# Expert matrices of a mixture layer: middle index numbered 11p + b, the last matrix read in rows of 12 KB

## The chip, the cores and the metric

The kernel runs on one core of a Trainium2 chip. The metric is the device time of one execution in microseconds. TensorE (PE in the profile) multiplies; its weight loads have a row of their own there (PEld). VectorE is DVE, ScalarE is ACT, GpSimd is POOL. SyncE (SP) issues all the weight loads of the part that is changed.

## The reference, cut to what matters

The program computes two layers of a hybrid trunk. The part that is changed is the feed-forward block of the second layer: a router picks two of eight experts for each of 256 tokens, and each expert is a SwiGLU with a middle width of 2816.

```python
def swiglu(h, w1, w3, w2):
    return jnp.matmul(jax.nn.silu(jnp.matmul(h, w1)) * jnp.matmul(h, w3), w2)

def moe_swiglu(h, router, w1, w3, w2):
    ...
    y = jnp.zeros_like(h)
    for e in range(N_EXPERTS):
        y = y + gates[..., e:e + 1].astype(h.dtype) * swiglu(h, w1[e], w3[e], w2[e])
    return y
```

`w1[e]` and `w3[e]` are 1024 x 2816 in float32, `w2[e]` is 2816 x 1024. The middle index (the 2816 columns of the first two, which are the 2816 rows of the last) is only summed over, so it may be taken in any order, as long as all three matrices use the same one.

## The kernel before

Everything up to the experts (two layers of mixing, the dense block of layer 0, the router) is left as it is. The experts run in a loop over rounds and, inside it, over the 8 experts; with these inputs there is one round. One expert is 24 pieces of weights, q = 0 to 23, that go through 8 slots `RAW` of 12 KB per partition, each with a slot `WLO` beside it:

- q 0 to 3 and 4 to 7: `w1` and `w3`, the first half of the middle index (1408 = 11 blocks of 128), two blocks of 128 rows of the matrix each, 128 x 2816 elements a piece; q 8 to 15: the same for the second half.
- q 16 to 23: `w2`, by `YBLOCKS`: six pieces of three blocks of 128 rows, then two of two blocks. A block has one row of 1024 floats (4 KB) in each partition.

For each piece, SP waits until the slot is free and issues the load (L1377 to L1393). DVE waits for the load and subtracts the upper half of each float, read as bfloat16 in place (`WHI`, every second 2-byte word), from the float; the rest goes to `WLO` as bfloat16 (L1547). PE then multiplies with both parts. DVE counts `m_lo` up for each piece and PE waits for it.

In `uv_piece` the weights of PE are 128 columns of the piece, one column of the middle index for each output row: `hi` columns lie 4 bytes apart, `lo` columns 2 bytes. There are 11 blocks x 2 rows x 3 products = 66 matmuls of 96 moving columns in a piece (L1429 and L1431 with `hi`, L1432 with `lo`), and 16 such pieces in an expert. In `y_piece` the hidden values are the weights (96 columns) and the piece is the moving operand, 512 columns at a time (L1451), 132 matmuls in an expert.

What else stands in the order: PE scatters the previous expert's output into token order after q 1 and q 3 (`pe_scatter`, L1409); DVE adds it to `Y` after its own q 3 and q 6 (`dve_add`, L1518). DVE forms the hidden values after q 9 and q 17 (`dve_hidden`, L1525 and L1527). PE gathers the next expert's tokens after q 17 (`pe_gather`, L1401). ACT copies the output (L1506) and takes silu (L1511). DVE copies a transposed gate and the next tokens after q 20 (L1565, L1496).

Of the kernel before, what the change touches and what calls it, by code (L numbers as in the profile page):

```python
# [35 lines left out]
P = 128  # L36
D = 1024
KC = D // P
# [84 lines left out]
def trunk(nc, t):  # L123
    ctx = ExitStack()
    with ctx:
# [35 lines left out]
        def B(i):  # L161
            return PS[:, i, :]
# [155 lines left out]
        for L in range(DEPTH):  # L318
# [4 lines left out]
            for g, key in enumerate(dict.fromkeys(u[0] for u in units)):  # L323
                c0, w = next((u[3], u[4]) for u in units if u[0] == key)
# [19 lines left out]
            if L == 0:  # L344
                for key in FFN_LOADS:
                    n = key[-1]
# [3 lines left out]
                    elif key[0] == "w2":  # L350
                        rows = min(4 * P, D_FF - 4 * P * n)
                        src = t["ffn_w2"][0][4 * P * n:4 * P * n + rows, :].rearrange("(c p) n -> p c n", p=P)
                        item(key, place, [(None, src)], ("ffn_y_mm", n + 1), split=True,
                             part=lambda v, r=rows // P: v[:, 0:2 * r, :])
                    else:
                        f0, w = FT[n]
# [883 lines left out]
        HALF, HB = D_FF // 2, FC // 2  # L1240
# [7 lines left out]
        HEH, HEL = HE[:, :, 0, :], HE[:, :, 1, :]  # L1248
# [96 lines left out]

        UBANK, VBANK, YBANK, GBANK, TBANK = 0, 3, 6, 0, 2
        GROUPS = [(0, 4), (4, 8), (8, HB)]
        YBLOCKS = [(3 * j, 3 * j + 3) for j in range(6)] + [(18, 20), (20, 22)]
        USED, FULL = 20, 12

        def uv_bank(bank0, b):

            return B(bank0 + b // 4)[:, SLOTS * (b % 4):SLOTS * (b % 4) + SLOTS]
# [21 lines left out]
        def sp_moe(sp):  # L1375
            for other in ENG:
                sp.wait_ge(S(f"{other}_stage_done"), MOE_STAGE)  # L1377

            def body(i, e):
                for q in range(NPIECE):  # L1380
                    sp_slot_free(sp, i, q)
                    if q < 16:
                        half, k = q // 8, 2 * (q % 4)
                        w = t["moe_w3" if q % 8 >= 4 else "moe_w1"][0, bass.ds(e, 1), P * k:P * k + 2 * P,
                                                                   HALF * half:HALF * half + HALF]
                        src = w.rearrange("a (k p) n -> p (a k) n", p=P)
                        dst = RAW[q % NSLOT][:, 0:2 * HALF].rearrange("p (k n) -> p k n", k=2)
                    else:
                        c0, c1 = YBLOCKS[q - 16]
                        w = t["moe_w2"][0, bass.ds(e, 1), P * c0:P * c1, :]  # L1390
                        src = w.rearrange("a (c p) n -> p (a c) n", p=P)
                        dst = RAW[q % NSLOT][:, 0:D * (c1 - c0)].rearrange("p (c n) -> p c n", n=D)
                    sp.dma_start(dst, src).then_inc(S(f"m_raw{q % NSLOT}"), 16)  # L1393
            rounds(sp, body)
# [25 lines left out]
        def pe_moe(pe):  # L1420
            def uv_piece(i, q, bank0):

                pe.wait_ge(S("m_lo"), NPIECE * i + q + 1)
                hi, lo = WHI[q % NSLOT], WLO[q % NSLOT]
                for n in range(2):
                    k = 2 * (q % 4) + n
                    for b in range(HB):
                        out, f = uv_bank(bank0, b), HALF * n + P * b
                        pe.matmul(out, hi[:, f:f + P], HEH[:, k, :], start=k == 0 and b % 4 == 0, stop=False,  # L1429
                                  skip_group_check=True)  # L1430
                        pe.matmul(out, hi[:, f:f + P], HEL[:, k, :], start=False, stop=False, skip_group_check=True)  # L1431
                        mm = pe.matmul(out, lo[:, f:f + P], HEH[:, k, :], start=False, stop=k == KC - 1,  # L1432
                                       skip_group_check=True)
                        if k == KC - 1 and b in (3, 7, HB - 1):
                            mm.then_inc(S("m_full"), 1)
                if q % 4 < 3:
                    mm.then_inc(S("m_used"), 1)
# [369 lines left out]
```

## Time and profile before

| | us |
|---|---|
| median of 3 runs | 2250.21 |
| lowest, highest | 2249.07, 2251.18 |
| profiled execution | 2252.25 |
| its span in the profile | 2250.5 |
| PE, DVE busy in the span | 1959.2, 1219.3 |
| the experts' part, first DVE piece to last PE piece | about 1532 to 2234 |
| one expert, from the third on | about 87.5 |

The times in the rows are microseconds from the start of the span, unless marked ns. A matmul's row lasts longer than its turn: the next one starts before it ends, so the turn is read from start to start. "Idle before" and the waits name what the engine waited for. The granted clock of PE is given as a share of 2.4 GHz. The chain at the page's end and the waits of one stretch serve to tell which engine holds the others up there.

### The profile page before, as it was taken

Reading aid. Unit: us, or ns where it says so; the run is one execution under the profiler, and the core shown is the slowest. Engines: PE = TensorE matmul, PEld = TensorE weight load, DVE = VectorE, ACT = ScalarE, POOL = GpSimd, SP = SyncE. Lnnn points to the kernel's source line nnn. Section 1 sums busy time; section 2 is a strip of 40 time slices with the busy share of each in tenths; the row PEclk is TensorE's granted clock in tenths of the full one; section 3 lists DMA queues with packets and bytes.
Section 4 is the critical chain, followed back from the end, with each engine's and each line's share of the span. In section 5 each row is a group of like instructions: output and inputs, shape, how many; then the busy total and the mean of one; then the engine's idle time right before and its main releaser. Section 6 shows DMA issues by size and latency. Waiting matters only on the chain.

```text
span 2250.5 us, 34491 instructions
## 1 busy us (share of the span) xinstructions
PE 1959.2 (87%) x15242; PEld 1248.2 (55%) x15242; DVE 1219.3 (54%) x1272; ACT 330.1 (15%) x555; POOL 177.0 (8%) x112
## 2 busy tenths in 40 slices
PE   2899997799779999797899858877999999999997
PEld 0333466756434444243444556646687687786774
DVE  1100327575352332222103475548999998989987
ACT  1200000043242222110100003321101101001000
POOL 0000505100000000000004450000000000000000
PEclk9899997855689999799999977578999999999999
DMA  8442210000144544412122100018999999999994
GB/s 275 174 169 103 74 49 1 1 1 1 38 150 169 202 153 161 175 57 75 38 75 75 56 0 1 1 38 360 411 411 413 410 399 396 410 397 401 404 390 162
DMA packets 121027, 409.34 MB, mean 182 GB/s; under 512 B 22168, under 2 KB 28952, under 8 KB 114736
## 3 DMA queue, kind: packets, MB, share of 16 engines
q1 hardware_dynamic: 112560, 405.57, 46.6%
q10 hardware_dynamic: 8320, 1.50, 0.6%
q8 instruction: 130, 2.13, 0.4%
q14 instruction: 17, 0.14, 0.0%
HBM read 406.01 MB, written 1.05 MB: 181 GB/s over the span
## 4 chain that ended last, share of the span: by engine, by line
PE 69%; DVE 18%; issue 5%; DMA 3%; ACTq 2%; ACT 2%; DVEq 1%; POOLq 1%; POOL 0%; PEldq 0%; SPq 0%; PEld 0%
PE PS L598 10%; PE PS L1165 10%; DVE ARENA L1547 10%; PE PS L596 8%; PE PS L1147 5%; PE PS L738 5%; PE PS L1429 4%; PE PS L1431 3%; PE PS L1432 3%; PE PS L1451 3%; PE PS L1084 3%; PE PS L969 2%; DMA ARENA<-in_moe_w 2%; ACTq L1645 2%; PE PS L445 2%
## 5 line engine op out<-in xcount | busy, mean ns | idle before, releaser
L1547 DVE TENSOR_TENSOR ARENA<-ARENA 128x2816 bf16<-128x2816 f32 (+1 forms) x192 | 581.5, 3084 | 5.8 <-DMA ARENA<-in_moe_w 3.8
L1429 PE MATMUL PS<-ARENA 128*128 128x96 bf16 x2816 | 376.1, 209 | 39.1 <-DVE ARENA L1547 33.4
L1431 PE MATMUL PS<-ARENA 128*128 128x96 bf16 x2816 | 375.4, 208 | 2.9 <-issue 2.9
L1432 PE MATMUL PS<-ARENA 128*128 128x96 bf16 x2816 | 375.4, 208 | 1.8 <-issue 1.7
L1429 PEld LDWEIGHTS PS<-ARENA 128*128 128x128 bf16 x2816 | 279.5, 99 | 53.3 <-DVE ARENA L1547 44.6
L1431 PEld LDWEIGHTS PS<-ARENA 128*128 128x128 bf16 x2816 | 279.7, 99 | 8.3 <-issue 8.3
L1432 PEld LDWEIGHTS PS<-ARENA 128*128 128x128 bf16 x2816 | 279.6, 99 | 3.1 <-issue 2.9
L1451 PE MATMUL PS<-ARENA 128*96 128x512 bf16 x1056 | 237.6, 384 | 2.9 <-DVE ARENA L1547 2.9
L598 PE MATMUL PS<-ARENA 128*128 128x512 f32 (+1 forms) x608 | 239.7, 554 | 0.0
L1165 PE MATMUL PS<-ARENA 128*128 128x512 bf16 x1056 | 232.6, 381 | 2.5 <-DVE ARENA L1197 2.5
L378 DVE TENSOR_TENSOR ARENA<-ARENA 128x4096 bf16<-128x4096 f32 (+1 forms) x26 | 91.4, 3522 | 227.5 <-ACT ARENA L372 227.4
L1451 PEld LDWEIGHTS PS<-ARENA 128*96 128x96 bf16 x1056 | 127.9, 122 | 106.4 <-issue 4.0
L629 DVE COPY ARENA<-PS 128x512 f32<-128x512 f32 (+1 forms) x32 | 19.9, 624 | 308.1 <-PE PS L598 308.1
L598 PEld LDWEIGHTS PS<-ARENA 128*128 128x128 f32 x608 | 116.2, 192 | 124.7 <-issue 121.4
L1165 PEld LDWEIGHTS PS<-ARENA 128*128 128x128 bf16 x1056 | 102.4, 98 | 136.0 <-issue 13.2
L596 PE MATMUL PS<-ARENA 128*128 128x512 f32 x384 | 169.7, 601 | 2.3 <-ACTq L395 2.3
L738 PE MATMUL PS<-ARENA 128*128 128x128 f32 x768 | 116.3, 326 | 53.6 <-issue 33.8
L738 PEld LDWEIGHTS PS<-ARENA 128*128 128x128 f32 x768 | 114.0, 241 | 56.3 <-issue 56.2
L596 PEld LDWEIGHTS PS<-ARENA 128*128 128x128 f32 x384 | 73.0, 192 | 97.5 <-issue 92.9
L1147 PE MATMUL PS<-ARENA 128*128 128x512 bf16 x528 | 117.0, 386 | 0.8 <-DVE GATE L483 0.8
L372 ACT ACTIVATE ARENA<-ARENA 128x4096 bf16<-128x4096 f32 (+1 forms) x26 | 74.9, 2890 | 149.1 <-PE PS L1147 85.5
L445 PE MATMUL PS<-ARENA,SC 128*32 128x512 f32 x384 | 48.9, 635 | 50.8 <-ACT SC L1650 44.0
(224 smaller groups left out, 1801.8 us busy)
## 6 DMA issues: line engine op xcount, KB each, us to landing
ARENA<-in_moe_w SPq DMA_DIRECT2D x128, 1408.0 KB, 12.9
ARENA<-in_moe_w SPq DMA_DIRECT2D x48, 1536.0 KB, 15.3
ARENA<-in_ada_w SPq DMA_DIRECT2D x24, 2048.0 KB, 7.7
ARENA<-in_ffn_w SPq DMA_DIRECT2D x15, 2048.0 KB, 7.9
ARENA<-in_w_in SPq DMA_DIRECT2D x12, 2048.0 KB, 8.0
ARENA<-in_moe_w SPq DMA_DIRECT2D x16, 1024.0 KB, 16.4
ARENA<-in_w_out SPq DMA_DIRECT2D x8, 1024.0 KB, 5.4
ARENA<-in_w_in SPq DMA_DIRECT2D x4, 1024.0 KB, 6.3
```

The lines of the kernel that those rows point to most:

```text
L378: dve.tensor_tensor(it["lo"], it["raw"], it["hi"], ALU.subtract).then_inc(S("split_lo"), 1)
L445: mm = pe.matmul(ps[32 * g:32 * g + 32, :], SC[:, 2 * kk + n, :], w[:, n, 512 * g:512 * g + 512], start=kk == 0 and n == 0, stop=False)
L596: mm = pe.matmul(B(bank), slot[:, k, P * u:P * u + P], HT[:, k, :], start=k == 0, stop=k == KC - 1)
L598: mm = pe.matmul(B(bank)[:, 0:w], HT[:, k, P * u:P * u + P], slot[:, k, 0:w], start=k == 0, stop=k == KC - 1)
L738: mm = pe.matmul(B(4 * d + h)[:, c], KE[d][:, h, c], q[:, h, c], start=True, stop=True)
L1147: mm = pe.matmul(B(2 * x + h), a[:, c, P * x:P * x + P], w[:, at:at + 512], start=c == 0 and n == 0, stop=c == FC - 1 and n == 2)
L1165: mm = pe.matmul(B(b0 + i % 3), w[:, k, P * c:P * c + P], x[:, k, :], start=k == 0 and w is hi and x is HTH, stop=k == KC - 1 and w is lo)
L1429: pe.matmul(out, hi[:, f:f + P], HEH[:, k, :], start=k == 0 and b % 4 == 0, stop=False, skip_group_check=True)
L1431: pe.matmul(out, hi[:, f:f + P], HEL[:, k, :], start=False, stop=False, skip_group_check=True)
L1432: mm = pe.matmul(out, lo[:, f:f + P], HEH[:, k, :], start=False, stop=k == KC - 1, skip_group_check=True)
L1451: mm = pe.matmul(B(YBANK + h)[0:SLOTS, :], x, y[:, at:at + 512], start=c == 0 and n == 0, stop=c == FC - 1 and n == 2)
L1547: dve.tensor_tensor(WLO[q % NSLOT][:, 0:n], RAW[q % NSLOT][:, 0:n], WHI[q % NSLOT][:, 0:n], ALU.subtract).then_inc(S("m_lo"), 1)
```

## The change

The 1408 middle indices of each half get another order. Before, block b held the 128 consecutive indices 128b to 128b + 127, index 128b + p in partition p. Now block b holds the indices 11p + b.

- For `w2`, partition p then needs rows 11p to 11p + 10 of the half, which lie one behind another in memory: 44 KB. A piece of three blocks is one run of 12 KB per partition, one of two blocks 8 KB, where before it was three or two runs of 4 KB. A piece may no longer reach over the border of the halves, so `YBLOCKS` becomes 3, 3, 3, 2 blocks in each half, in place of 3, 3, 3, 3, 3, 3, 2, 2.
- For `w1` and `w3` the loads stay. The weights of a matmul are now every 11th column of the piece: `hi` 44 bytes apart, `lo` 22 bytes.

The numbers of matmuls, DVE operations, loads and bytes are the same.

```diff
-        YBLOCKS = [(3 * j, 3 * j + 3) for j in range(6)] + [(18, 20), (20, 22)]
+        YBLOCKS = [(HB * half + a, HB * half + min(a + 3, HB)) for half in range(2) for a in range(0, HB, 3)]
...
                         c0, c1 = YBLOCKS[q - 16]
-                        w = t["moe_w2"][0, bass.ds(e, 1), P * c0:P * c1, :]
-                        src = w.rearrange("a (c p) n -> p (a c) n", p=P)
+                        half = c0 // HB
+                        w = t["moe_w2"][0, bass.ds(e, 1), HALF * half:HALF * half + HALF, :]
+                        src = w.rearrange("a (p c) n -> p (a c) n", p=P)[:, c0 - HB * half:c1 - HB * half, :]
...
-                        out, f = uv_bank(bank0, b), HALF * n + P * b
-                        pe.matmul(out, hi[:, f:f + P], HEH[:, k, :], start=k == 0 and b % 4 == 0, stop=False,
+                        out, f = uv_bank(bank0, b), slice(HALF * n + b, HALF * n + HALF, HB)
+                        pe.matmul(out, hi[:, f], HEH[:, k, :], start=k == 0 and b % 4 == 0, stop=False,
                                   skip_group_check=True)
-                        pe.matmul(out, hi[:, f:f + P], HEL[:, k, :], start=False, stop=False, skip_group_check=True)
-                        mm = pe.matmul(out, lo[:, f:f + P], HEH[:, k, :], start=False, stop=k == KC - 1,
+                        pe.matmul(out, hi[:, f], HEL[:, k, :], start=False, stop=False, skip_group_check=True)
+                        mm = pe.matmul(out, lo[:, f], HEH[:, k, :], start=False, stop=k == KC - 1,
                                        skip_group_check=True)
```

The order changes only at the pieces of `w2`. On PE, at the end of an expert's body (L1451 before and L1452 after are `y_piece`, L1401 and L1402 the gather; every number of a line below the diff's is one higher after). Before:

```order
L1451 MATMUL PS<-ARENA 96x512 x18
L1440 REGISTER_ALU
L1451 MATMUL PS<-ARENA 96x512 x18
L1440 REGISTER_ALU
L1451 MATMUL PS<-ARENA 96x512 x18
L1440 REGISTER_ALU
L1451 MATMUL PS<-ARENA 96x512 x18
L1440 REGISTER_ALU
L1451 MATMUL PS<-ARENA 96x512 x12
L1440 REGISTER_ALU
L1451 MATMUL PS<-ARENA 96x512 x12
```

After, the same six pieces behind the gather:

```order
L1452 MATMUL PS<-ARENA 96x512 x18
L1441 REGISTER_ALU
L1452 MATMUL PS<-ARENA 96x512 x12
L1441 REGISTER_ALU
L1452 MATMUL PS<-ARENA 96x512 x18
L1441 REGISTER_ALU
L1452 MATMUL PS<-ARENA 96x512 x18
L1441 REGISTER_ALU
L1452 MATMUL PS<-ARENA 96x512 x18
L1441 REGISTER_ALU
L1452 MATMUL PS<-ARENA 96x512 x12
```

One of the two short pieces has moved from fifth place (q 22) to second (q 19) of these six. On DVE, from the hidden values of the second half to the loop's end (L1547 and L1548 are the subtraction, L1565 and L1566 the gate's copy, L1496 and L1497 the tokens). Before:

```order
L1527 TENSOR_TENSOR ARENA<-ARENA 128x1056
L1547 TENSOR_TENSOR ARENA<-ARENA 128x3072 x3
L1565 COPY M<-PS 96x256
L1495 ISA
L1496 TENSOR_TENSOR ARENA<-PS,ARENA 128x4x96
L1495 REGISTER_ALU
L1496 TENSOR_TENSOR ARENA<-PS,ARENA 128x4x96
L1547 TENSOR_TENSOR ARENA<-ARENA 128x3072
L1547 TENSOR_TENSOR ARENA<-ARENA 128x2048 x2
```

After:

```order
L1528 TENSOR_TENSOR ARENA<-ARENA 128x1056
L1548 TENSOR_TENSOR ARENA<-ARENA 128x3072
L1548 TENSOR_TENSOR ARENA<-ARENA 128x2048
L1548 TENSOR_TENSOR ARENA<-ARENA 128x3072
L1566 COPY M<-PS 96x256
L1496 ISA
L1497 TENSOR_TENSOR ARENA<-PS,ARENA 128x4x96
L1496 REGISTER_ALU
L1497 TENSOR_TENSOR ARENA<-PS,ARENA 128x4x96
L1548 TENSOR_TENSOR ARENA<-ARENA 128x3072 x2
L1548 TENSOR_TENSOR ARENA<-ARENA 128x2048
```

The copy and the tokens stand one block (1024 elements) earlier than before.

## Rows read from the trace of the kernel before

**Rows 1.** The page, part 1: busy time, share of the span, instructions.

```profile
PE 1959.2 (87%) x15242; PEld 1248.2 (55%) x15242; DVE 1219.3 (54%) x1272; ACT 330.1 (15%) x555; POOL 177.0 (8%) x112
```

**Rows 2.** Busy time by stretch: one expert (the fifth), columns in the first line.

```profile
core 0: us, PE busy (x) PEld busy (x) DVE busy (x) ACT busy (x) POOL busy (x), PEclk, DMA share, GB/s
...
1877.80:1965.30 87.50, 82.48 (x1232) 65.77 (x1230) 81.75 (x44) 7.20 (x12) 0.00 (x0) 0.98 1.01 401
```

**Rows 3.** Waits, 1500 to 2250: engine, line, for what; us, times, longest.

```profile
DVE X L1518 <- PE PS L1409: 34.8, 14, 5.5
PE PS L1429 <- DVE ARENA L1547: 33.4, 22, 5.9
...
DVE ARENA L1547 <- DMA ARENA<-in_moe_w: 3.8, 10, 0.5
...
SPq L1393 <- PE PS L1432: 352.1, 124, 6.6
```

**Rows 4.** The same waits, only those for a DMA, 1530 to 1700.

```profile
DVE ARENA L1547 <- DMA ARENA<-in_moe_w: 3.4, 9, 0.5
```

**Rows 5.** DVE in order of time: start, length, operation, idle before.

```profile
1870.10 19.76 DVE L1547 TENSOR_TENSOR ARENA<-ARENA 128x3072 bf16<-128x3072 f32 x7
1895.37 0.69 DVE L1518 TENSOR_TENSOR X<-PS,X 128x512 f32<-128x512 f32 x1 [5.51 <-PE PS L1409]
...
1896.84 9.09 DVE L1547 TENSOR_TENSOR ARENA<-ARENA 128x2816 bf16<-128x2816 f32 x3
```

**Rows 6.** The same, one expert later.

```profile
1982.90 0.69 DVE L1518 TENSOR_TENSOR X<-PS,X 128x512 f32<-128x512 f32 x1 [5.47 <-PE PS L1409]
1983.76 0.69 DVE L1518 TENSOR_TENSOR X<-PS,X 128x512 f32<-128x512 f32 x1 [0.17 <-PE PS L1409]
1984.37 3.08 DVE L1547 TENSOR_TENSOR ARENA<-ARENA 128x2816 bf16<-128x2816 f32 x1
```

**Rows 7.** Busy time by stretch (columns as in rows 2) over that expert's chain.

```profile
1896.00:1941.00 45.00, 42.51 (x930) 40.27 (x928) 44.80 (x26) 2.57 (x6) 0.00 (x0) 1.00 1.01 401
1941.00:1972.00 31.00, 31.00 (x166) 17.60 (x166) 30.97 (x17) 2.27 (x3) 0.00 (x0) 1.00 1.02 409
1972.00:1974.50 2.50, 0.07 (x1) 0.00 (x0) 2.50 (x2) 2.36 (x3) 0.00 (x0) 1.00 1.00 394
```

**Rows 8.** PE in order of time, around the start of the next expert.

```profile
1974.56 0.21 PE L1429 MATMUL PS<-ARENA 128*128 128x96 bf16 x1 [2.48 <-DVE ARENA L1547]
...
1981.78 1.95 PE L1409 MATMUL PS<-GATE,M 96*128 96x512 f32 x4
1983.56 0.21 PE L1429 MATMUL PS<-ARENA 128*128 128x96 bf16 x1
```

**Rows 9.** PE, first and last of 69 matmuls in a row at the full clock.

```profile
1800.07 0.21 PE L1429 MATMUL PS<-ARENA 128*128 128x96 bf16 x1 [2.60 <-DVE ARENA L1547]
...
1802.96 0.21 PE L1432 MATMUL PS<-ARENA 128*128 128x96 bf16 x1
```

**Rows 10.** Durations by line, ns: min/median/max, first and last start, form.

```profile
L1429 PEld LDWEIGHTS PS<-ARENA x2816: 96/98/145, 1535.2 to 2202.2; 128*128 128x128 bf16 x188
...
L1432 PEld LDWEIGHTS PS<-ARENA x2816: 95/98/145, 1535.2 to 2202.2; 128*128 128x128 bf16 x188
...
L1451 PEld LDWEIGHTS PS<-ARENA x1056: 121/122/126, 1591.6 to 2233.4; 128*96 128x96 bf16 x176
L1451 PE MATMUL PS<-ARENA x1056: 377/387/429, 1591.6 to 2233.6; 128*96 128x512 bf16 x176
```

**Rows 11.** PE in order of time: 13 float32 matmuls of 128 columns, merged.

```profile
329.76 1.61 PE L738 MATMUL PS<-ARENA 128*128 128x128 f32 x13
```

**Rows 12.** Durations of line 738 on PE, ns: min/median/max.

```profile
L738 PE MATMUL PS<-ARENA x768: 274/275/553, 320.2 to 1348.4; 128*128 128x128 f32 x192
```

**Rows 13.** Busy time by stretch (columns as in rows 2): loads of w1, w3, then w2.

```profile
1530.00:1532.00 2.00, 0.00 (x0) 0.00 (x0) 0.39 (x1) 0.36 (x1) 0.00 (x0) 1.00 1.02 428
...
1888.00:1905.00 17.00, 17.00 (x299) 14.90 (x297) 11.32 (x6) 1.28 (x3) 0.00 (x0) 0.92 0.96 365
1905.00:1927.30 22.30, 21.10 (x489) 20.66 (x487) 22.27 (x13) 0.40 (x1) 0.00 (x0) 1.00 1.02 415
1927.30:1955.80 28.50, 27.21 (x369) 20.59 (x367) 28.47 (x17) 3.15 (x6) 0.00 (x0) 1.00 1.02 408
```

## The prediction

> **What bounds the kernel now.** The page's first part gives PE 87% of the span and DVE 54% [rows 1], an average over stages; only the experts are changed, so the first view to open is the busy time of one expert. In 87.5 us PE is busy 82.48, DVE 81.75, and the DMA share is 1.01 [rows 2]. Three resources look full, and the change touches two of them: it could give the DMA something and take something from PE. Which one sets the time is told by the waits. DVE waits for a load only 3.8 us in the whole stage [rows 3], 3.4 of it before 1700, that is in the first two experts [rows 4]; it waits 34.8 us for PE's scatter (L1409), and PE waits 33.4 us for DVE's subtraction. SP waits 352.1 us for slots that PE has not freed. So the loads are ahead: the DMA is busy because it runs nearly at the pace of the loop, but it doesn't set that pace.
>
> The order of time shows the loop. DVE idles 5.51 us before its add at 1895.37, then starts q 4 at 1896.84 [rows 5]; one expert later it idles 5.47 us before the add and starts q 4 at 1984.37 [rows 6]. That is 87.53 us from q 4 to q 4, in two parts. (a) 1896.8 to 1941: DVE works without a gap (44.80 of 45.00 us) and PE follows it [rows 7]. (b) 1941 to 1984: PE's w2 pieces, back to back for 31.0 us; 2.5 us in which PE goes round the loop [rows 7]; q 0 and q 1, 1974.56 to 1981.78; the scatter of 1.8 us; then DVE's two adds [rows 6, 8]. DVE has done its pieces 0 to 3 long before and waits. The chain is DVE for one half and PE for the other; no load is in it.
>
> **The turn of one matmul.** 69 matmuls of `uv_piece` start between 1800.07 and 1802.96 [rows 9]: 2.89 / 68 = 42.5 ns each, at the 2.4 GHz level. 96 moving columns at one per cycle are 40 ns. So the moving operand sets the turn and the weight load lies under it. A piece of 66 takes 2.8 us, against 3.0 for DVE's subtraction (9.09 us for three [rows 5]). This closeness is what the change puts at risk.
>
> **Part 1: w2 in runs of 12 KB.** The w2 loads of this expert took about 28.5 us at 408 GB/s; the stretch with w1 and w3, whose runs are 5.6 KB, shows 415 [rows 13]. The nearest row for a gain by longer runs is the step from 4 to 5.6 KB, 408 to 415: 0.5 us of an expert. The upper end is the best rate in any row, 428 in a short stretch: 28.5 x (1 - 408/428) = 1.3 us. The lower end is a loss, if 128 streams 44 KB apart read memory less well; the worst row of this stretch, 365 GB/s, would make 28.5 into 31.9, a loss of 3.4. I take a gain of 0.5 to 1 us of DMA time. On the path it is worth nothing, since no load is on it: even in the first two experts all of DVE's waits for a DMA are 3.4 us [rows 4], for the loads of all three matrices, and whatever DVE gains there ends before the wait for the scatter. Cover: the wait for PE's scatter, 5.5 us in each expert. **Value taken: 0.**
>
> **Part 2: pieces of w2 in another order.** A short piece moves from q 22 to q 19. The sum on PE and DVE is the same, and PE runs through (b) without a wait after the first 0.4 us. DVE's copy and tokens come one block, some 1.1 us, earlier; PE needs them 15 us later. SP's waits are by piece number and a slot is freed at most 1.4 us earlier or later. **0.**
>
> **Part 3: weights 44 and 22 bytes apart.** 1056 weight loads per expert, 8448 in all. No row of before has weights more than 4 bytes apart, so the price is bounded.
> - The rows within reach: `hi` (4 bytes) and `lo` (2 bytes) both take 98 ns [rows 10], so doubling the step cost nothing there. The w2 matmuls read the piece as moving operand: 387 ns, with a minimum of 377 [rows 10]. One product in three reads `lo` and two read `hi`, so I read the 10 ns as what the 4-byte step costs over 512 columns, an estimate: a step isn't always free.
> - How much room a load has: the load of 96 columns takes 122 ns, of 128 columns 98 [rows 10]. The 128-column form is thus a faster one. If 96 columns go one per cycle (40 ns), the fixed part is 82, and the fast load itself lasts about 16 ns (estimate). It may become 2.6 times as long before it reaches the turn of 42.5.
> - Lower end: nothing. Upper end: the float32 matmuls of L738, whose weights have no fast form. 13 of them take 1.61 us, the last one 0.275 [rows 11, 12]: (1.61 - 0.275) / 12 = 111 ns a turn. Half of it, 55.5 ns, is a plain load of 128 columns at one per cycle (53 ns) with the 2.5 ns that the turn of 42.5 has over its 40.
>
> From turn to time: let d be what the turn grows by. q 0 and q 1 (132 matmuls) lie in (b) and cost 132 d. The 14 pieces in (a) (924 matmuls) take 14 x 2.81 + 1.8 for a scatter = 41.1 of the 45.0 us, so 3.9 us are free; they cost 924 d - 3.9 us, if that is above nothing, that is from d = 4.2 ns on.
>
> Here the Trainium skill speaks on both sides. The SBUF page (SBUF — State Buffer, on SBUF "cachelines" in Door 1) says that the memory is read in lines of 16 bytes, that two hits on a line are needed to hide its latency, and that each access to a new line costs; both new steps put every weight on a line of its own. That rule speaks against the change; no run here shows its size. TensorE: Matmul & The Clock Gate (Weight-path perf modes) lets the fast load be used with columns up to 1,024 elements apart, and 22 is well inside; by that the fast form stays.
>
> I take the fast form as kept and its 16 ns as at most doubled, to 32: still under 42.5, so d = 0. The row it is nearest to is `hi` against `lo`, 98 and 98. **Value taken: 0.**
>
> **Sum.** 2252.25 us for the profiled execution, less 0, plus 0. The median of the runs is 2250.21, 2.0 lower than the profiled one, so I predict 2250.
>
> **The rivals.**
> - R1, slower: the load loses the fast form or runs at a quarter of it, and the turn becomes 55.5 ns. d = 13.0: 132 d = 1.7, 924 d - 3.9 = 8.1; 9.8 us per expert, 79 us: 2329. For it: a new line for each weight, and 10 ns seen in the moving operand at only 4 bytes. Against: the ratio of 2.6 that the load has to spare. It decides from d = 4.2 ns, a turn of 46.7.
> - R2, much slower: the slower memory adds to a plain load, or the four parts of a fast load get in each other's way, and the turn is the 111 ns of L738. d = 68.5: 9.0 + 59.4 = 68.4 us per expert, 547 us: 2797. PE would never wait and DVE would wait for it at every piece.
> - R3, slightly slower: the reads of weights on many lines get in the way of DVE's reads or of PE's own moving operand, a turn of 44 to 48 ns. At 48, 0.7 + 1.2 = 1.9 us per expert, 15 us: 2265. The same size results if the w2 loads lose 3.4 us per expert, since the DMA is nearly at the loop's pace (2.4 us more than it could hide, seven times, 17 us: 2267).
> - R4, faster: the loads set the pace after all (share 1.01). Then the gain of part 1 counts, 0.5 to 1.3 us, eight times: 4 to 10 us, 2240 to 2246. Against: only 3.8 us of waits for a DMA in the stage [rows 3].
> - That the change doesn't do what it says is excluded for the loads, since the load's pattern on SP is one row of 3072 elements in place of three of 1024, unless the hardware cuts these rows again. That falls together with the forecast.
>
> **How the numbers follow.** A difference of over 0.2%, 4.5 us, is about what a measurement of this kernel can tell. Forecast (within 4.5 us of 2250): 0.45. R1: 0.22. R2: 0.14. R3: 0.11. R4: 0.08. So faster 0.08, same 0.45, slower 0.47. The likeliest single case is no change; with signs on both sides its own range is 2246 to 2254. The range to hold 8 in 10 starts at 2244, takes in R3 and R1 with a little above it for its bounds, 2340, and leaves out R2 and the far part of R4.
>
> **What would show it.** The turn of the matmuls of the three lines (42.5 ns if right) and the median of their weight loads (98 now, 114 if doubled and hidden; above 125 they can't be hidden). DVE's wait for the scatter, 34.8 us now: larger if PE is slower. PE's wait for the subtraction, 33.4 us now: gone if the turn passes 46 ns. The rate in w2's stretches, 408 GB/s now: 415 and more if longer runs help; the time stays all the same. The prediction is wrong if the weight load outgrows the moving operand, and that is the step I am least sure of.

## The result and the profile after

| | before | after |
|---|---|---|
| median, us | 2249.64 (2246.78 to 2251.18) | 2392.59 (2389.77 to 2393.12) |
| profiled execution, us | 2252.25 | 2393.12 |
| its span | 2250.5 | 2391.4 |
| ratio of the times | | 1.0634, 95% interval 1.0616 to 1.0653 |

The changed kernel is 143 us slower, 17.9 us for each of the eight experts. The prediction of 2250 was wrong, and its range ended at 2340.

The page of after, part 1, to set beside [rows 1]: PE has 156.4 us more, weight loads 171.5 more, DVE 7.8 more. The number of operations of DVE, ACT and POOL is the same.

```profile
PE 2115.6 (88%) x15201; PEld 1419.7 (59%) x15242; DVE 1227.1 (51%) x1272; ACT 332.0 (14%) x555; POOL 178.1 (7%) x112
```

Durations by line of after, in ns (min/median/max), to set beside [rows 10]. `L1430` and `L1432` are the two products with `hi`, `L1433` the one with `lo`, `L1452` is `y_piece`:

```profile
L1430 PEld LDWEIGHTS PS<-ARENA x2816: 141/161/173, 1538.0 to 2343.5; 128*128 128x128 bf16 x188
...
L1432 PEld LDWEIGHTS PS<-ARENA x2816: 141/168/181, 1538.0 to 2343.6; 128*128 128x128 bf16 x188
...
L1433 PEld LDWEIGHTS PS<-ARENA x2816: 136/161/174, 1538.1 to 2343.6; 128*128 128x128 bf16 x188
...
L1452 PEld LDWEIGHTS PS<-ARENA x1056: 121/122/142, 1609.7 to 2374.2; 128*96 128x96 bf16 x176
L1452 PE MATMUL PS<-ARENA x1056: 377/387/393, 1609.8 to 2374.4; 128*96 128x512 bf16 x176
```

The weight loads of the three changed lines went from 98 to 161 and 168 ns, beyond the 125 named in the prediction as the point past which they can't be hidden. `y_piece`, whose operands didn't change, has the same medians as before, 122 and 387. So nothing slowed PE as a whole.

The turn is read from start to start, PE of after in order of time at the full clock:

```profile
1700.00 0.23 PE L1432 MATMUL PS<-ARENA 128*128 128x96 bf16 x1
1700.07 0.22 PE L1433 MATMUL PS<-ARENA 128*128 128x96 bf16 x1
1700.12 0.23 PE L1430 MATMUL PS<-ARENA 128*128 128x96 bf16 x1
...
1702.49 0.23 PE L1432 MATMUL PS<-ARENA 128*128 128x96 bf16 x1
```

From 1700.00 to 1702.49 there are 39 turns: 2.49 / 39 = 63.8 ns, where [rows 9] has 42.5. A piece of 66 takes 4.2 us in place of 2.8, and DVE's subtraction still 3.0. PE is now the slower one in both halves of the loop. The waits from 1500 to the end, columns as in [rows 3]:

```profile
DVE ARENA L1526 <- PE PS L1433: 92.2, 24, 6.3
DVE X L1519 <- PE PS L1410: 76.8, 16, 11.8
...
PE PS L1430 <- DVE ARENA L1548: 12.4, 4, 5.9
```

DVE waits 76.8 us for the scatter (34.8 before) and, in a new wait, 92.2 us for the last matmuls of a group, before it forms the hidden values. PE's wait for the subtraction fell from 33.4 to 12.4 us. The loop in DVE's order of time, two experts, to set beside [rows 5, 6]:

```profile
1862.71 0.69 DVE L1519 TENSOR_TENSOR X<-PS,X 128x512 f32<-128x512 f32 x1 [10.26 <-PE PS L1410]
...
1889.52 1.67 DVE L1526 TENSOR_TENSOR ARENA<-PS,ARENA 128x384 f32<-128x384 f32 x3 [6.05 <-PE PS L1433]
...
1923.13 0.56 DVE L1526 TENSOR_TENSOR ARENA<-PS,ARENA 128x384 f32<-128x384 f32 x1 [5.25 <-PE PS L1433]
...
1967.47 0.69 DVE L1519 TENSOR_TENSOR X<-PS,X 128x512 f32<-128x512 f32 x1 [10.50 <-PE PS L1410]
```

From add to add it is 104.76 us, 87.53 before. DVE now idles three times for long in an expert (10.3, 6.1 and 5.3 us in the first three rows; the fourth is the next expert's). The half that DVE led before, (a) in the prediction, has passed to PE. Busy time by stretch (columns as in [rows 2]), first one whole expert, then the parts of another: its pieces q 4 to 15 (780 of their 792 matmuls), `w2`, the turn of the loop, q 0 and q 1 with the scatter:

```profile
1840.40:1944.90 104.50, 102.18 (x1232) 86.69 (x1231) 82.38 (x45) 7.42 (x12) 0.00 (x0) 1.00 0.91 334
```

```profile
1873.58:1923.30 49.72, 49.72 (x780) 49.72 (x778) 38.29 (x22) 1.40 (x3) 0.00 (x0) 1.00 0.91 327
1923.30:1954.80 31.50, 31.50 (x182) 18.49 (x181) 31.24 (x17) 2.27 (x3) 0.00 (x0) 1.00 0.94 353
1954.80:1957.20 2.40, 0.47 (x4) 0.01 (x1) 2.17 (x1) 1.88 (x3) 0.00 (x0) 1.00 0.98 359
1957.20:1968.12 10.92, 10.92 (x136) 9.92 (x137) 0.65 (x1) 0.48 (x1) 0.00 (x0) 0.84 0.88 319
```

PE is busy 102.18 of 104.50 us; what is left is the turn of the loop. The DMA rate fell from 401 to 334 GB/s. That is a result and no cause: the same bytes are spread over a longer expert, SP waits for slots that PE frees later, and no DVE wait for a DMA is left in the view of waits. The mean rate tells only the pace of the loop here.

### The profile page after: what moved, and what is told of

It is laid out like the page before. It is cut to its first block, busy times and chain, and to the rows that moved or that the text cites. A ratio compares the mean times of both kernels' runs of the same rounds, so it can differ in the third digit from the quotient of the medians.

```text
span 2391.4 us, 34450 instructions
## 1 busy us (share of the span) xinstructions
PE 2115.6 (88%) x15201; PEld 1419.7 (59%) x15242; DVE 1227.1 (51%) x1272; ACT 332.0 (14%) x555; POOL 178.1 (7%) x112
## 4 chain that ended last, share of the span: by engine, by line
PE 79%; DVE 12%; issue 3%; ACTq 2%; ACT 2%; DMA 1%; DVEq 1%; POOLq 0%; POOL 0%; PEldq 0%; SPq 0%; PEld 0%
PE PS L598 10%; PE PS L1165 10%; PE PS L1430 8%; PE PS L1432 8%; PE PS L1433 7%; PE PS L596 7%; DVE ARENA L1548 6%; PE PS L1147 5%; PE PS L738 5%; PE PS L1452 4%; PE PS L1084 3%; PE PS L969 2%; ACTq L1646 2%; PE PS L445 2%; PE PS L958 1%
## 5 line engine op out<-in xcount | busy, mean ns | idle before, releaser
L1548 DVE TENSOR_TENSOR ARENA<-ARENA 128x2816 bf16<-128x2816 f32 (+1 forms) x192 | 580.4, 3082 | 1.7 <-issue 1.6
L1430 PE MATMUL PS<-ARENA 128*128 128x96 bf16 x2816 | 544.9, 231 | 21.6 <-DVE ARENA L1548 12.4
L1432 PE MATMUL PS<-ARENA 128*128 128x96 bf16 x2816 | 545.0, 231 | 0.0
L1433 PE MATMUL PS<-ARENA 128*128 128x96 bf16 x2816 | 544.9, 224 | 0.0
L1432 PEld LDWEIGHTS PS<-ARENA 128*128 128x128 bf16 x2816 | 474.9, 169 | 4.6 <-issue 4.6
L1430 PEld LDWEIGHTS PS<-ARENA 128*128 128x128 bf16 x2816 | 455.6, 162 | 28.8 <-issue 14.9
L1433 PEld LDWEIGHTS PS<-ARENA 128*128 128x128 bf16 x2816 | 455.9, 162 | 0.0
L1452 PE MATMUL PS<-ARENA 128*96 128x512 bf16 x1056 | 237.3, 384 | 0.0
L1165 PE MATMUL PS<-ARENA 128*128 128x512 bf16 x1032 | 230.1, 381 | 4.5 <-DVE ARENA L1197 2.7
L1452 PEld LDWEIGHTS PS<-ARENA 128*96 128x96 bf16 x1056 | 128.1, 122 | 102.3
L1165 PEld LDWEIGHTS PS<-ARENA 128*128 128x128 bf16 x1056 | 102.4, 98 | 136.0 <-issue 13.2
L738 PE MATMUL PS<-ARENA 128*128 128x128 f32 x768 | 114.7, 323 | 59.3 <-issue 32.5
L738 PEld LDWEIGHTS PS<-ARENA 128*128 128x128 f32 x768 | 112.4, 238 | 62.1 <-issue 62.0
L1147 PE MATMUL PS<-ARENA 128*128 128x512 bf16 x517 | 114.5, 382 | 1.7 <-DVE GATE L483 1.2
```

The lines of the kernel that those rows point to most:

```text
L738: mm = pe.matmul(B(4 * d + h)[:, c], KE[d][:, h, c], q[:, h, c], start=True, stop=True)
L1147: mm = pe.matmul(B(2 * x + h), a[:, c, P * x:P * x + P], w[:, at:at + 512], start=c == 0 and n == 0, stop=c == FC - 1 and n == 2)
L1165: mm = pe.matmul(B(b0 + i % 3), w[:, k, P * c:P * c + P], x[:, k, :], start=k == 0 and w is hi and x is HTH, stop=k == KC - 1 and w is lo)
L1430: pe.matmul(out, hi[:, f], HEH[:, k, :], start=k == 0 and b % 4 == 0, stop=False, skip_group_check=True)
L1432: pe.matmul(out, hi[:, f], HEL[:, k, :], start=False, stop=False, skip_group_check=True)
L1433: mm = pe.matmul(out, lo[:, f], HEH[:, k, :], start=False, stop=k == KC - 1, skip_group_check=True)
```

## Experiments

The theory after the result: the loss is the weight load, which takes longer where the columns lie further apart, has outgrown the moving operand, and sets the turn. Rivals: the long runs of `w2` (memory read with 44 KB between partitions), the new order of the pieces, or reads of the weights that collide with DVE's. "Turn" is start to start at the full clock, unless said otherwise. A turn is named by the matmul that it begins with, and is set beside the weights of that matmul.

### Which half of the change it is: runs_only and steps_only

`runs_only` is the changed kernel with contiguous weights:

```diff
-                        out, f = uv_bank(bank0, b), slice(HALF * n + b, HALF * n + HALF, HB)
+                        out, f = uv_bank(bank0, b), slice(HALF * n + P * b, HALF * n + P * b + P)
```

> The w2 loads and YBLOCKS of the changed kernel, weights of w1 and w3 read as before (128 neighbouring columns); the sum then pairs middle indices of different matrices, so only its time is of use. Theory A (all of the loss is PE's weight loads, which set the turn of the matmuls): turn 42.5 ns, time of before within 5 us, 2250, although the w2 loads run at 415 to 428 GB/s. Rival B (the loads set the pace): 2240 to 2246. Rival C (runs of 12 KB with 44 KB between them read memory less well and carry part of the 142 us; the rate of the loads in the changed kernel is only 320 to 350 GB/s): above 2265, up to 2390.

Measured: 2249.66 us, ratio to before 0.9994, interval 0.9983 to 1.0004. The stretch of `w2` loads that answers to the last of [rows 13] shows 418 GB/s instead of 408:

```profile
1927.30:1955.80 28.50, 27.21 (x368) 20.55 (x366) 28.47 (x19) 3.10 (x6) 0.00 (x0) 1.00 1.01 418
```

and in the stretch from 1700 to 2200 a `w2` piece of three blocks lands 12.4 us after its issue, 14.3 before. Here first `runs_only`, then before (KB each, median us to landing):

```profile
ARENA<-in_moe_w SPq DMA_DIRECT2D x36, 1536.0 KB, 12.4
ARENA<-in_moe_w SPq DMA_DIRECT2D x11, 1024.0 KB, 12.0
```

```profile
ARENA<-in_moe_w SPq DMA_DIRECT2D x36, 1536.0 KB, 14.3
ARENA<-in_moe_w SPq DMA_DIRECT2D x11, 1024.0 KB, 15.0
```

The long runs do what they say: the loads are faster, by 2.4% in this stretch. The rate is the better sign of it. The time to landing holds queueing too, since the pieces of `w1` and `w3`, whose runs are the same, also land earlier, 9.8 us after their issue for 11.1. The time doesn't move, since no load is on the chain. Nor does the new order of pieces, which this run has as well, cost anything that can be seen. Both rivals fall as causes of the loss.

`steps_only` is the other half, the strided weights with `YBLOCKS` and `w2` as before:

```diff
-        YBLOCKS = [(HB * half + a, HB * half + min(a + 3, HB)) for half in range(2) for a in range(0, HB, 3)]
+        YBLOCKS = [(3 * j, 3 * j + 3) for j in range(6)] + [(18, 20), (20, 22)]
...
-                        half = c0 // HB
-                        w = t["moe_w2"][0, bass.ds(e, 1), HALF * half:HALF * half + HALF, :]
-                        src = w.rearrange("a (p c) n -> p (a c) n", p=P)[:, c0 - HB * half:c1 - HB * half, :]
+                        w = t["moe_w2"][0, bass.ds(e, 1), P * c0:P * c1, :]
+                        src = w.rearrange("a (c p) n -> p (a c) n", p=P)
```

> The weights of the changed kernel (44 and 22 bytes apart) with the w2 loads and YBLOCKS of before; the sum again pairs different indices. Theory A: the turn averages 63.5 ns, 104.8 us per expert, 2390 to 2395. Rival C: below 2380, with the rest in the runs_only kernel.

Measured: 2395.67 us, ratio 1.0631 (1.0608 to 1.0653), the same as the whole change. Its loads too:

```profile
L1429 PEld LDWEIGHTS PS<-ARENA x2816: 141/161/176, 1533.7 to 2345.5; 128*128 128x128 bf16 x188
```

All of the loss is the step of the weights.

### One step at a time: hi44_lo2 and hi4_lo22

```diff
-                        out, f = uv_bank(bank0, b), HALF * n + P * b
-                        pe.matmul(out, hi[:, f:f + P], HEH[:, k, :], start=k == 0 and b % 4 == 0, stop=False,
+                        out, f, g = uv_bank(bank0, b), slice(HALF * n + b, HALF * n + HALF, HB), slice(HALF * n + P * b, HALF * n + P * b + P)
+                        pe.matmul(out, hi[:, f], HEH[:, k, :], start=k == 0 and b % 4 == 0, stop=False,
```

with `lo[:, g]` in the third product; `hi4_lo22` has the two slices the other way round.

> Before, with only the hi weights 44 bytes apart, lo contiguous (hi and lo then belong to different indices: time only). The two loads of hi and the one of lo in a row. Theory A1 (a load costs by the 16-byte lines that it touches; with 44 and 22 bytes both touch one line per weight): the turns that the hi loads set are about 65 ns, the one that lo sets is 42.5: mean 57.5, about 98.5 us per expert, 2340. Theory A2 (only the number of bytes between weights counts, or hi is slow since it starts at the odd half of a word): lo would be different from hi in the changed kernel too.

> Before, with only the lo weights 22 bytes apart, hi 4 bytes apart as before. A1: one turn of three about 60 to 65 ns, mean 49: 66 x 49 = 3.2 us for a piece, just over DVE's 3.0; in the part where PE follows DVE 924 x 6.5 = 6.0 us less 3.9 free, and 132 x 6.5 = 0.9: 3 us per expert, 2274. If lo alone costs nothing: 2250.

Measured: `hi44_lo2` 2354.2 us in one execution, an expert of 100.7 us; `hi4_lo22` 2266.8, likewise in one, an expert of about 89. The loads of the three lines, first `hi44_lo2`, then `hi4_lo22`:

```profile
L1429 PEld LDWEIGHTS PS<-ARENA x2816: 141/143/161, 1534.8 to 2304.5; 128*128 128x128 bf16 x188
...
L1431 PEld LDWEIGHTS PS<-ARENA x2816: 142/168/183, 1534.8 to 2304.6; 128*128 128x128 bf16 x188
...
L1432 PEld LDWEIGHTS PS<-ARENA x2816: 98/122/145, 1534.9 to 2304.6; 128*128 128x128 bf16 x188
```

```profile
L1429 PEld LDWEIGHTS PS<-ARENA x2816: 96/113/145, 1538.6 to 2217.2; 128*128 128x128 bf16 x188
...
L1431 PEld LDWEIGHTS PS<-ARENA x2816: 96/98/145, 1538.7 to 2217.3; 128*128 128x128 bf16 x188
L1432 PEld LDWEIGHTS PS<-ARENA x2816: 134/137/158, 1538.7 to 2217.3; 128*128 128x128 bf16 x188
```

The turns are 64, 67 and 43 ns in the one (a mean of 58, d = 15.7) and 43, 43 and 57 in the other (48, d = 5). Only the turns that begin with a matmul whose own weights are strided are long, and the two effects add up. By the prediction's formula, 132 d + (924 d - 3.9 us), d = 15.7 gives 12.7 us per expert or 2354 us, and d = 5 gives 1.4 us or 2263. Both are within 4 us of what came. So the step from turn to time holds at these two sizes, and it is the turn that was missed. That `hi4_lo22` is so cheap is the 3.9 us of free time of the DVE half.

### The load by itself: sweep16, sweep96, sweep16_quiet

`sweep16` gives each of the 11 blocks its own step and cuts the moving operand of all three products to 16 columns, so that little hides the load (of the edit, the lines for the first product):

```diff
-                        out, f = uv_bank(bank0, b), HALF * n + P * b
-                        pe.matmul(out, hi[:, f:f + P], HEH[:, k, :], start=k == 0 and b % 4 == 0, stop=False,
+                        out, f = uv_bank(bank0, b)[:, 0:16], slice(HALF * n, HALF * n + (P - 1) * (b + 1) + 1, b + 1)
+                        pe.matmul(out, hi[:, f], HEH[:, k, 0:16], start=k == 0 and b % 4 == 0, stop=False,
```

> The kernel of before, with two edits: block b takes 128 columns of the piece b + 1 elements apart (the same columns are then used more than once and others left out), and only 16 of the 96 moving columns are multiplied. The turn then shows the weight load alone, without the 42.5 ns that 96 columns hide. Steps 1 to 11 give hi at 4, 8, ... 44 bytes, lo at 2, 4, ... 22. Theory L (a load is paid by 16-byte lines): the turn after hi grows up to step 4 (16 bytes) and is flat from there, near 60 to 65 ns; the turn after lo grows up to step 8 and is flat from there. Theory F (the fast form is lost as soon as the columns don't neighbour): a jump between step 1 and 2 to about 55, then flat. Theory G (cost grows with the distance without end): still rising between 8 and 11 for both. Step 1 gives what a load costs in the kernel of before: 16 to 20 ns if the estimate from the durations (98 and 122) was right.

`sweep96` has the same steps with all 96 columns:

> The same steps by block with all 96 moving columns (columns are used twice or left out, as in sweep16). The turn is the larger of 42.5 ns and the load, in each theory. L: 42.5 up to step 2 for hi (8 lines of 16 bytes in each row of 16 weights, half a line each), above it from step 3 or 4 on; for lo 42.5 up to step 4. F: 55 for every step but 1.

`sweep16_quiet` is `sweep16` with DVE's subtraction cut to 64 of its 2816 or 3072 elements, and `hi` in the place of `lo` in every product:

> sweep16 with DVE's subtraction cut to 64 elements of each piece and all three products made with hi (the low parts are left out). It asks whether the price of a far step is PE's own or comes from DVE reading and writing the same memory at the same time. Own: hi turns as in sweep16, 25, 35, 48, 66, 58 and about 60 to 65 ns for steps 1 to 11. Shared: clearly lower beyond step 2.

One row of blocks of `sweep16` at the full clock, from PE in order of time (start, length). Three matmuls for each block, and each block's step is one element longer than the last one's:

```profile
1629.77 0.17 PE L1431 MATMUL PS<-ARENA 128*128 128x16 bf16 x1
1629.79 0.17 PE L1432 MATMUL PS<-ARENA 128*128 128x16 bf16 x1
1629.82 0.18 PE L1429 MATMUL PS<-ARENA 128*128 128x16 bf16 x1
1629.86 0.18 PE L1431 MATMUL PS<-ARENA 128*128 128x16 bf16 x1
...
1630.04 0.21 PE L1429 MATMUL PS<-ARENA 128*128 128x16 bf16 x1
1630.10 0.21 PE L1431 MATMUL PS<-ARENA 128*128 128x16 bf16 x1
1630.17 0.18 PE L1432 MATMUL PS<-ARENA 128*128 128x16 bf16 x1
...
1631.24 0.21 PE L1429 MATMUL PS<-ARENA 128*128 128x16 bf16 x1
1631.31 0.21 PE L1431 MATMUL PS<-ARENA 128*128 128x16 bf16 x1
1631.37 0.20 PE L1432 MATMUL PS<-ARENA 128*128 128x16 bf16 x1
```

The view rounds to 10 ns: the first block's turns from 1629.77 on are 20 and 30; the fourth block's (`hi` 16 bytes apart) are 60 and 70; the last one's (44 bytes) 70 and 60. Medians of the turns at the full clock, read from the traces to the nanosecond (in `sweep16` only 2 to 6 turns for each step and product, and 3 to 8 in the quiet kernel, since the clock was mostly lower there; in `sweep96` about 250):

| step of the weights, bytes | 16-byte lines under 128 weights | `sweep16`, ns | `sweep96`, ns |
|---|---|---|---|
| 2, 4, 6 (2 and 6 `lo`) | 16, 32, 48 | 25, 25, 26 | 42 to 43 |
| 8 | 64 | 33 to 36 | 42 |
| 10 (`lo`) | 80 | 38 | 42 |
| 12 | 96 | 46 to 49 | 46 to 47 |
| 14 (`lo`) | 112 | 54 | 55 |
| 16 | 128 | 63 (`lo`), 66 (`hi`) | 62, 64 |
| 18 to 22 (18, 22 `lo`) | 128 | 58 to 60 | 58 to 61 |
| 24 to 40 (`hi`) | 128 | 58 to 63 | 60 to 64 |
| 44 (`hi`) | 128 | 64 to 67 | 67 to 70 |

A number of bytes gives the same turn whether it is reached with `hi` or with `lo` (8 bytes: 34 to 36 and 33). The turns go with the number of lines of 16 bytes that the 128 weights of a partition lie on: 0.48 ns a line (62 / 128) fits 38 ns at 80 lines, 47 at 96 and 54 at 112 (at 64 lines it gives 31 for a measured 33 to 36), with a floor of 25, which may be that of so short a matmul and not the load's. Beyond 16 bytes each weight has its own line, and the price is flat but for the 64 to 70 ns at 44 bytes. The first turn of a row of blocks, which follows the last block's far step, is left out of the 25: it was 37 in the median. `sweep96` shows max(42.5, load): a load of up to 38 ns is hidden by 96 columns, one of 47 is not.

The price does not go with TensorE's clock. For most of `sweep16` the granted clock was 0.50, the level of 1.2 GHz:

```profile
1730.00:1790.00 60.00, 60.00 (x1035) 55.50 (x1035) 48.46 (x26) 2.78 (x6) 0.00 (x0) 0.50 0.92 350
```

With about 250 turns for each step at that level, the medians are 26 to 28 ns at 2 and 4 bytes, 29 at 6, 32 to 35 at 8, 40 at 10, 47 to 48 at 12, 55 at 14, 62 to 64 at 16, 58 to 63 from 18 to 40 and 65 at 44: the table's values, beyond the floor to within 2 or 3 ns. A load of one column per cycle would have taken 128 / 1.2 = 107 ns there.

Beside it stands the rule that the prediction named, from the Trainium skill (SBUF — State Buffer, on cachelines in Door 1): memory is read in lines of 16 bytes, and two hits on a line absorb the latency. The line size shows as a plateau from 16 bytes on. The other half doesn't show: at 8 bytes there are two weights on a line and the load is already 10 ns longer than at 4. For this load the measured price goes by the line.

In the quiet kernel the turns are 25, 34 to 36, 46 to 47, 61 to 62, 58, 59, 60 to 61, 62 to 63, 62, 60 and 67 to 69 ns for the 11 steps, as in `sweep16`, while DVE is nearly still. Busy time by stretch of that kernel, DVE in the third place after the length:

```profile
1700.00:1800.00 100.00, 97.68 (x1229) 78.25 (x1227) 13.59 (x41) 7.42 (x12) 0.00 (x0) 0.65 0.91 345
```

DVE is busy 13.59 of 100 us, before 81.75 of 87.5 [rows 2]. So the price isn't contention with DVE. Nor is it contention with the DMA, which wrote at 345 GB/s on the whole but not evenly. In the quiet kernel there are stretches with neither, and the turns stay: over 500 turns at steps of 20 bytes and more, begun in half microseconds with under 150 GB/s, have a median of 62 ns, as have those with over 300. Here is such a stretch, 3 us for 58 matmuls of all steps; behind it two of the changed kernel, with little DMA and with much, 35 matmuls each:

```profile
1656.50:1659.50 3.00, 3.00 (x58) 3.00 (x56) 0.00 (x0) 0.00 (x0) 0.00 (x0) 0.50 0.14 19
```

```profile
1763.00:1765.00 2.00, 2.00 (x35) 2.00 (x34) 2.00 (x1) 0.00 (x0) 0.00 (x0) 1.00 0.54 84
1765.00:1767.00 2.00, 2.00 (x35) 2.00 (x34) 2.00 (x2) 0.58 (x2) 0.00 (x0) 1.00 0.82 327
```

The times of these kernels (2331.42, 2321.15 and 2354.61 us, one execution each) say little: in the two with 16 columns the granted clock was 0.795 and 0.792 over the core against 0.897 before.

### Where in the loop the price counts: steps_q01 and steps_q89

The prediction's formula says that strided weights in two pieces of (b) cost 132 d = 2.8 us per expert, and in two pieces of (a) nothing, since 3.9 us are free there. Both kernels have the same number of slow loads:

```diff
-                        out, f = uv_bank(bank0, b), HALF * n + P * b
+                        out = uv_bank(bank0, b)
+                        f = (slice(HALF * n + b, HALF * n + HALF, HB) if q in (0, 1) else slice(HALF * n + P * b, HALF * n + P * b + P))
```

and `q in (8, 9)` in the second.

> Before, with the weights 44 and 22 bytes apart only in pieces q 0 and 1 of each expert (132 matmuls that DVE's wait for the scatter depends on); the middle indices of these pieces don't fit the others, so only the time is of use. Slow turns cost 132 x 21 ns = 2.8 us per expert. Chain theory (q 0 and 1 lie where PE alone holds the chain): all of it comes out, 8 x 2.8 = 22 us, 2272. Pool theory (PE simply has about 4 us to spare per expert, wherever it is): 2250.

> The same 2.8 us per expert, but in pieces q 8 and 9, where PE follows DVE and is 1.5 us and less behind it (time only, as in steps_q01). Chain theory: PE is idle 3.9 us in that half, so the lateness is made good before q 16: 2250 to 2255. Pool theory: 2250.

Measured: `steps_q01` 2262.1 us, ratio 1.0059 (1.0039 to 1.0079); `steps_q89` 2251.76, ratio 1.0001 (0.999 to 1.0012). The waits of DVE for the scatter, first `steps_q01`, then `steps_q89` (34.8 before [rows 3]):

```profile
DVE X L1519 <- PE PS L1409: 49.2, 16, 8.0
```

```profile
DVE X L1519 <- PE PS L1409: 36.2, 14, 6.3
```

The place decides, as the chain says: the same 132 slow turns cost 10 to 13 us in one half (2262.1 against 2251.7 of before in the same rounds, or the ratio) and nothing in the other. The size in (b) was too high: in the traces an expert from the second on is 1.9 us longer, for an expected 2.8. The reason is that q 0 and q 1 of before lose some time already, in one of two forms. In four of the seven experts after the first, the clock falls to half (the level of 1.2 GHz) for most of q 0, shortly after the 2.5 us in which PE goes round the loop. In the other three it stays at 1.00. Busy time by stretch, one expert of before in the first form, then one of `steps_q01` at the full clock:

```profile
1887.00:1889.00 2.00, 1.98 (x26) 1.98 (x27) 2.00 (x1) 0.00 (x0) 0.00 (x0) 0.54 1.02 422
1889.00:1891.00 2.00, 2.00 (x33) 2.00 (x31) 0.86 (x1) 0.00 (x0) 0.00 (x0) 0.61 1.01 411
```

```profile
1885.40:1887.40 2.00, 2.00 (x32) 2.00 (x33) 2.00 (x1) 0.00 (x0) 0.00 (x0) 1.00 1.04 428
1887.40:1889.40 2.00, 2.00 (x35) 2.00 (x34) 0.80 (x1) 0.00 (x0) 0.00 (x0) 1.00 1.04 417
```

At half the clock a turn is 80 ns (96 / 1.2), and it stays 80 with strided weights, since their 59 to 67 ns lie under it. So q 0 goes only from 4.4 us to 4.9 in this form, and q 1 from 2.8 to 4.2. At the full clock q 0 goes from 2.8 to 4.2, but q 1 only from 3.8 to 4.2: in before it has a gap of 1.0 to 1.1 us in its middle for which the profile names no cause, and with slower turns this gap isn't there. Together q 0 and q 1 go from 7.2 to 9.1 us in the one form and from 6.6 to 8.4 in the other, 1.9 in both. In `steps_q01` three of the seven later experts have the halved stretch. Why an expert falls into the one form or the other, the runs don't tell.

### Keeping the long runs: groups

If lines are what costs, a smaller step keeps the runs without the loss. `groups` numbers the middle index 3p + c inside each group of three blocks (2p + c in the last two of a half). A `w2` piece is still one run of 12 or 8 KB, and the weights lie 12 and 6 bytes apart (8 and 4 in the last two blocks):

```diff
-                        src = w.rearrange("a (c p) n -> p (a c) n", p=P)
+                        src = w.rearrange("a (p c) n -> p (a c) n", p=P)
...
-                        out, f = uv_bank(bank0, b), HALF * n + P * b
+                        g, m = 3 * (b // 3), min(3, HB - 3 * (b // 3))
+                        out = uv_bank(bank0, b)
+                        f = slice(HALF * n + P * g + b - g, HALF * n + P * (g + m), m)
```

with `YBLOCKS` of the changed kernel, and with `hi[:, f]` and `lo[:, f]` in the products.

> A version meant to keep the long runs at a smaller step: the middle index is numbered 3p + c within each group of three blocks (2p + c in the last two), so that each w2 piece is one run of 12 KB (8 KB) per partition and the weights lie 12 and 6 bytes apart (8 and 4 in the last two blocks). Everything is computed. Theory L: a hi load touches 96 lines in place of 128, three quarters of 65 ns: a turn of 43 to 50, lo hidden: mean 43 to 47.5, 2250 to 2280. Theory F: as steps_only less a little, 2350 to 2390. The runs themselves give nothing (runs_only).

Measured: 2250.28 us, ratio 1.0002 (0.9993 to 1.0012). `hi` turns of 45 to 46 ns, `lo` 43, a piece of 2.93 us for 2.81: d = 2, which the 3.9 us hide. Its loads (the three lines are `L1431`, `L1433`, `L1434` there):

```profile
L1431 PEld LDWEIGHTS PS<-ARENA x2816: 111/125/148, 1536.1 to 2203.9; 128*128 128x128 bf16 x188
...
L1434 PEld LDWEIGHTS PS<-ARENA x2816: 97/108/146, 1536.1 to 2204.0; 128*128 128x128 bf16 x188
```

The 125 are also just the bound that the prediction gave for a load that can't be hidden: the turn is 3 ns longer there. All values are computed in this kernel, so it does what the change was for, without the loss; but it gains nothing over before either.

### Is there anything for faster loads to give: adds_later and groups_later

DVE idles 5.5 us in each expert for the scatter [rows 5, 6]. `adds_later` puts its adds after q 5 and 7:

```diff
-                    if q == 3:
+                    if q == 5:
...
-                    if q == 6:
+                    if q == 7:
```

> The kernel of before with the two adds of dve_add after DVE's pieces 5 and 7 in place of 3 and 6, everything computed. It takes away DVE's 5.5 us wait for the scatter in each expert, if the chain through both engines is the bound as read from before. That chain then loses up to 5.5 us, until the loads bind at 34.6 MB / 413 GB/s = 83.8 us per expert in place of 87.5: 2220 to 2232. If the loads had been the bound all along: 2250.

`groups_later` is `groups` with the same edit:

> groups and adds_later together, everything computed. In adds_later PE has hardly any idle time left (86.3 us per expert), so the turn of 45.5 ns that steps of 12 bytes give to the hi loads, free in groups, must now be paid: 9 of 11 blocks x 2 of 3 turns x 3 ns = 1.8 ns on 1056 matmuls = 1.9 us per expert, 15 us more than adds_later: 2250 to 2262. If the runs of 12 KB give something once the adds are later (loads as the bound): below 2246.

Measured: `adds_later` 2246.57 us, ratio 0.9987 (0.9975 to 0.9999); `groups_later` 2251.99, ratio 1.0004 (0.9994 to 1.0014). The first is the fastest of all the kernels run here, by 0.13%, and its interval only just leaves out 1; the 18 to 30 us expected didn't come. Waits of `adds_later`, then of `groups_later`:

```profile
DVE ARENA L1525 <- PE PS L1432: 29.1, 8, 3.9
```

```profile
DVE ARENA L1527 <- PE PS L1434: 32.8, 8, 4.3
```

The wait for the scatter is nearly gone (1.8 us in all), and DVE waits for the last matmuls of the first half in its place, 3.6 us on average. An expert takes 86.4 us from the third on, for 87.3 in before. PE needs nearly that long for its own work: of 87.50 us it was busy 82.48 in before [rows 2], and 2.5 more are the turn of the loop. I took DVE's idle time for what could be won, and PE had only some 2.5 us to spare. In `adds_later` PE still stands for 1.9 to 3.3 us of an expert in gaps inside `uv_piece` for which the profile names no cause, so what holds it up there is open. The first expert is even 3.3 us longer (93.6 for 90.3), since PE waits 3.4 us for the add there. In `groups_later` the slower turn of 45 to 46 ns has less left to hide under and takes the 4 us back, fewer than the 15 expected; the runs of 12 KB give nothing even here.

## Why the prediction was wrong, point by point

- **What bounds the kernel: held.** The loop of two halves, no load in it. Half of the change acted on the loads, made them faster, and moved nothing (`runs_only`).
- **Part 1, the long runs: held.** A gain of 0.5 to 1 us of DMA time was taken; 418 for 408 GB/s over 28.5 us is 0.7. On the path 0, as measured. The fear of 128 streams 44 KB apart, a loss of 3.4 us, is not borne out.
- **Part 2, the order of the pieces: held**, 0.
- **Part 3, the step that failed.** "I take the fast form as kept and its 16 ns as at most doubled, to 32." The second number, the doubling, had no row at all, and it is what failed: at 22 and 44 bytes the loads set turns of 59 and 64 to 67 ns, beyond the 42.5 of the moving operand, where 32 would have been hidden. The 16 was worked out as 98 less a fixed part of 82, which came from another form of load (96 columns, 122 ns) under an assumption of one column per cycle. No run shows it: with 16 moving columns the turn didn't go below 25 ns, so the load takes 25 or less. From 25 to 59 is 2.4 times, from 16 to 67 over 4 times. The "ratio of 2.6 that the load has to spare" is sure only as 42.5 / 25 = 1.7. The row that it leaned on, `hi` against `lo` at 98 and 98, couldn't bear it: 2 and 4 bytes are 16 and 32 lines, and both turns are at the floor. The two rows said that a small step is free, and nothing on a large one.
- **R1: the right mechanism, mis-sized.** It had the load as what sets the turn, at 55.5 ns, and the turn is 63.8. The number was a plain load of one column per cycle, half of L738's float32 turn, and lay near by luck: such a load would take 107 ns at the halved clock, where `sweep16` shows 58 to 65, as at the full one. What goes with the load's time is lines. 8.3 ns on the turn is 8.8 us per expert, 70 us in all; that covers the 64 by which R1's 2329 fell short. R1 had the load lose its fast form or run at a quarter of it. The first is not what happened, as far as the fast form means more than one column per cycle; and a turn that grows smoothly from 8 to 16 bytes speaks against a switch at some step.
- **From turn to time: held in the main.** With d = 63.8 - 42.5 = 21.3 it gives 2.8 + 19.7 - 3.9 = 18.6 us per expert, 149 us; 143 were measured. The term that was too high is the first: q 0, q 1 and the scatter went from a mean of 8.8 us to 10.7, 2.0 and not 2.8, for the reason given with `steps_q01`.
- **R2** (111 ns) fell with the same turn. **R3** had as its cause reads of weights that get in the way of DVE's or of PE's own moving operand. `sweep16_quiet` excludes the first as the cause of the price; against the second speaks that the far steps have the same turns with 16 moving columns as with 96. Its other cause, the DMA near the loop's pace, played no part either: no wait of DVE for a load is left in the changed kernel. **R4** fell with `runs_only`.
- **The chances.** 0.45 stood on the value 0 in a place where the range of the unknown price was 0 to 68.5 ns and no sign at hand gave its size. With no row at all beyond a step of 4 bytes, most of the chance belonged with the rivals in which the load shows.

## What to carry to other kernels

A load of 128 bf16 weights cost here by the 16-byte lines that it reads in a partition, and the same at both levels of TensorE's clock. At up to 3 elements of step it allowed a turn of 25 to 29 ns, from 8 elements on it took 58 to 70 ns. To hide that at the full clock, a moving operand of some 140 to 165 columns is needed; this is an estimate from the 42.5 ns of 96 columns and the 215 of 512 (0.42 to 0.44 ns a column), no run tried it. Where a layout in memory asks for a stride, make it the smallest that gives the long run (here 3 and not 11), and first ask whether a load is on the chain at all; here it wasn't. Idle time of one engine is worth only what the other engine of the loop has to spare.

## What the hardware showed that was not expected

- Steps of exactly 16 bytes are a little dearer than those of 18 to 22: 63 and 66 ns against 58 to 60, with 96 columns 62 and 64 against 58 to 61, and without DVE's work 61 to 62 against 58 (at the lower clock, with 250 turns each, 60 to 61 against 58 to 61). At 44 bytes it is 64 to 70. The cause wasn't looked for.
- The duration of a weight load in the profile isn't its turn. The record grew from 98 to 161 ns and more (+63) while the turn grew by 21 on average, and 125 ns in the record meant a turn of 45 to 46. What is left over is time in which the load waits or overlaps.
- A moving operand with a step isn't free either. In `y_piece` of before, the products that read `lo` (2 bytes apart) last 377 ns and have a turn of 215, those that read `hi` (4 bytes apart) 387 and 225 to 227, medians for 512 columns. The prediction had estimated these 10 ns from the minimum and the median of [rows 10]; product by product the trace bears it out.
- Runs of 12 KB read faster than those of 4 KB: 418 against 408 GB/s in the same stretch of an expert.
